# Out-projection operands built inside the last attention turn, and two output tiles started on their attention half, in a hybrid attention and state-space decoder step

## The reference, cut to what matters

```
att = att_fn(q, k, v, qi, wi, ki)
...
y = rmsnorm(y.reshape(B, T, SSM_WIDTH) * jax.nn.silu(z), ssm_norm)
h = x + jnp.concatenate([att, y], axis=-1) @ w_out
f = rmsnorm(h, norm_ffn)
h = h + (jax.nn.silu(f @ w_gate) * (f @ w_up)) @ w_down
```

## Time and profile before

| | |
|---|---|
| median of 3 runs | 3020.83 us (3015.36 to 3022.0) |
| the profiled execution | 3024.53 us, span 3022.4 us |
| PE busy | 2830.1 us (94%) |
| DVE, ACT, POOL busy | 1508.8, 949.1, 548.8 us |
| turn 8 and start of the out-projection | about 1120 to 1223 us of the span |
| DMA | 354.00 MB, mean 117 GB/s |

### The profile page before, as it was taken

The page is one execution under the profiler, slowest core; times in us unless marked ns, Lnnn a source line. Parts: engine busy times, 40 slices in busy tenths (PEclk is TensorE's granted clock), DMA queues, the critical chain, the costliest instruction groups (busy, mean ns, idle before and its releaser), DMA issues.

```text
span 3022.4 us, 49649 instructions
## 1 busy us (share of the span) xinstructions
PE 2830.1 (94%) x20713; PEld 2694.1 (89%) x20713; DVE 1508.8 (50%) x2311; ACT 949.1 (31%) x1440; POOL 548.8 (18%) x230
## 2 busy tenths in 40 slices
PE   6999999999999986997899999999999999999997
PEld 5887898877777764996899999999999999999997
DVE  3312399544444445015766776766766633232223
ACT  4222221232333323223334344343333422222222
POOL 2222232211111100431000000000000033333331
PEclk9999999999999987998899999999999999999999
DMA  6422222555555545442232333333333352323221
GB/s 203 115 72 73 72 77 78 147 150 159 158 148 150 152 119 189 131 131 80 78 110 96 128 100 98 121 100 115 105 100 119 116 200 100 115 100 116 100 100 63
DMA packets 367372, 354.00 MB, mean 117 GB/s; under 512 B 40957, under 2 KB 321125, under 8 KB 365880
## 3 DMA queue, kind: packets, MB, share of 16 engines
q1 hardware_dynamic: 334136, 325.20, 34.0%
q10 hardware_dynamic: 33024, 25.77, 2.6%
HBM read 303.18 MB, written 49.13 MB: 117 GB/s over the span
## 4 chain that ended last, share of the span: by engine, by line
PE 57%; issue 31%; POOL 7%; DVE 2%; ACTq 1%; ACT 1%; POOLq 0%; DVEq 0%
PE PS L1230 32%; PE PS L1212 19%; PE PS L789 6%; POOL WL L692 4%; POOL WL L721 3%; ACTq L1274 0%; DVE XR L2264 0%; ACTq L1275 0%; DVE xo_t L2269 0%; DVE xo_x L2269 0%; DVE y_out L2339 0%; POOL WL L713 0%; ACT WRAW L1283 0%; DVE rstd L2257 0%; PE PS L804 0%
## 5 line engine op out<-in xcount | busy, mean ns | idle before, releaser
L789 PE MATMUL PS<-AH,WH 128*128 128x288 f32 (+1 forms) x2208 | 497.6, 308 | 30.1 <-DVE AL L2164 11.0
L1212 PE MATMUL PS<-H,WH 128*128 128x288 f32 x2816 | 489.5, 296 | 0.7 <-DVE us L2231 0.7
L789 PE MATMUL PS<-AL,WH 128*128 128x288 f32 (+1 forms) x2208 | 483.8, 302 | 0.0
L789 PE MATMUL PS<-AH,WL 128*128 128x288 f32 (+1 forms) x2208 | 482.3, 301 | 0.0
L711 POOL TENSOR_TENSOR WL<-WRAW,WH 128x1024 fp32r<-128x1024 f32 x88 | 213.9, 2431 | 1379.6 <-ACT WH L704 1379.6
L789 PEld LDWEIGHTS PS<-AH,WH 128*128 128x128 f32 (+1 forms) x2208 | 366.8, 195 | 56.4 <-issue 35.1
L1212 PEld LDWEIGHTS PS<-H,WH 128*128 128x128 f32 x2816 | 414.6, 189 | 0.9 <-issue 0.9
L1230 PE MATMUL PS<-xo_t,WH 128*128 128x288 f32 x1888 | 380.9, 296 | 7.8 <-ACT kept L1627 7.6
L789 PEld LDWEIGHTS PS<-AL,WH 128*128 128x128 f32 (+1 forms) x2208 | 367.0, 194 | 0.0
L789 PEld LDWEIGHTS PS<-AH,WL 128*128 128x128 f32 (+1 forms) x2208 | 365.5, 194 | 0.0
L2325 DVE TENSOR_TENSOR XD<-PS,XD 128x576 f32<-128x576 f32 x176 | 133.4, 758 | 398.8 <-PE PS L1212 398.8
(11 more groups left out here) (351 smaller groups left out, 3786.2 us busy)
## 6 DMA issues: line engine op xcount, KB each, us to landing
WRAW<-in_w_gate SPq DMA_DIRECT2D x22, 2048.0 KB
WRAW<-in_w_up SPq DMA_DIRECT2D x22, 2048.0 KB
WRAW<-in_w_down SPq DMA_DIRECT2D x22, 2048.0 KB
WRAW<-in_w_in SPq DMA_DIRECT2D x14, 2048.0 KB, 8.4
raw<-in_w_in SPq DMA_DIRECT2D x48, 512.0 KB, 4.1
kca<-in_cache_k SPq DMA_DIRECT2D x256, 64.0 KB, 2.8
vca<-in_cache_v SPq DMA_DIRECT2D x256, 64.0 KB, 2.0
WRAW<-in_w_out SPq DMA_DIRECT2D x16, 1024.0 KB
```

The source lines that it names most:

```text
L789: last = nc.tensor.matmul(G[gslot][0:width, h, 0:HALF], wt[:, half, k % 8, 0:width], act[:, (k + shift) % KT, h * HALF:(h + 1) * HALF], st ...
L1212: last = mm(G[(slot + t) % 2][:, h, 0:HALF], wt[:, half, 2 * k + t, :], hid[:, m, k, h * HALF:(h + 1) * HALF], start=(k == 0 and wt is WH ...
```

## The change

`mx` gets 16 places and lies where `AL` lies, so each low part is written over its own input. That memory is free once the last q, k, v product has been read (`w_used` at C3). In turn 8, SP issues two loads of seven rows each, attention rows 0 to 6 and SSM rows 8 to 14, between values 3 and keys 2. Rows 15 and 7 are loaded singly after the turn. ACT (`mix_high`) and DVE (`mix_low`) build the parts of rows 0 to 6 inside turn 8. After the turn ACT makes the first two weight halves, then row 7's high part, then the root, then rows 8 to 15. PE computes the attention halves of tiles 0 and 1 first, and then their SSM halves, as `ATT_FIRST` says.

```
-        mx = sb("mx", [P, 6, NT], at=spot["bf"][0])
+        mx = sb("mx", [P, KT, NT], at=spot["AL"][0])
...
+        ATT_FIRST = (0, 2, 1, 3)
...
+            def load_mix(n, lo, hi):
+                sp.dma_start(mx[:, lo:hi, :], mixS[lo:hi].rearrange("k p n -> p k n")).then_inc(mx_in[n], 16)
...
             def turn_sp(i, att=True, units=True, mamba=True, more=True):
                 a = i - 1
                 for n in range(6):
+                    if n == 2 and not units:
+                        sp.wait_ge(s["w_used"], C3)
+                        sp.wait_ge(s["mixa"], 16 * 7)
+                        load_mix(0, 0, 7)
+                        sp.wait_ge(s["ymix"], 16 * 7)
+                        load_mix(1, 8, 15)
...
             sp.wait_ge(s["hout"], 16 * 8)
             load_w(0, out_cols(0), 0)
             sp.wait_ge(s["ymix"], 16 * 8)
+            load_mix(3, 15, 16)
+            twait(sp, "pvs", 8)
+            load_w(1, out_cols(1), 1)
+            sp.wait_ge(s["mixa"], 16 * NH)
+            load_mix(2, 7, 8)
...
-            sp.wait_ge(s["mixa"], 16 * 7)
-            for j in range(6):
-                load_mix(j)
-            twait(sp, "pvs", 8)
-            load_w(1, out_cols(1), 1)
...
-            for j in range(6, KT):
-                load_mix(j)
...
-            for n in range(KT):
+            for d, (n, h) in enumerate(((0, 0), (1, 0), (0, 1), (1, 1))):
+                if d < 2:
+                    pe.wait_ge(s["tile_taken"], T3 + n - 1)
+                ready = (lambda k: pe.wait_ge(s["mix_lo"], k + 1)) if n == 0 else None
+                half_unit(pe, C3 + d, h, (T3 + n) % 2, ready=ready, slot=d % 2)
+            for n in range(2, KT):
...
+            def mix_high(j):
+                act.wait_ge(mx_in[{7: 2, 15: 3}.get(j, j // 8)], 16)
+                if j >= 8:
+                    act.wait_ge(s["y_norm"], j - 7)
+                copy(AH[:, j, :], mx[:, j, :]).then_inc(s["m_hi"], 1)
...
-            hi_p(C3, 0, 0)
-            hi_p(C3 + 1, 1, 0)
...
+            hi_p(C3, 0, 0, 0)
+            hi_p(C3 + 1, 2, 0, 1)
+            mix_high(7)
+            for h in range(2):
+                wait(act, f"ssy{h}")
+                taken(actv(rstd[:, h, :], bank(f"ssy{h}")[:, 0:HALF], ACT.Sqrt, bias=eps[:, :], scale=1.0 / (NM * DS)), f"ssy{h}")
+            for j in range(8, KT):
+                mix_high(j)
...
             for c in range(2, 32):
-                hi_p(C3 + c, c % 4, c // 4)
+                if c < 4:
+                    hi_p(C3 + c, ATT_FIRST[c], 0, c % 2)
+                else:
+                    hi_p(C3 + c, c % 4, c // 4)
...
+            def mix_low(j):
+                dve.wait_ge(s["m_hi"], j + 1)
+                tt(AL[:, j, :], mx[:, j, :], AH[:, j, :].bitcast(F32), ALU.subtract).then_inc(s["mix_lo"], 1)
...
+            mix_low(7)
+            for h in range(2):
+                given(dve, f"ssy{h}")
+            dve.wait_ge(s["tile_taken"], T3)
+            nc.vector.reciprocal(rstd[:, :, :], rstd[:, :, :]).then_inc(s["ry_done"], 1)
+            dve.wait_ge(s["ry_done"], 1)
+            for j in range(8, KT):
+                y_norm(j)
+                if j > 8:
+                    mix_low(j - 1)
+            mix_low(KT - 1)
```

More of the change, by code:

```diff
@@ L242, in build @@
         w_ld = [sem(f"w_ld{t}") for t in range(2)]
-        mx_in = [sem(f"mx_in{t}") for t in range(6)]
+        mx_in = [sem(f"mx_in{t}") for t in range(4)]
         xt_in = [sem(f"xt_in{t}") for t in range(2)]
@@ L586, in out_cols @@
                 return src
[L588 to L594, removed]
             def load_x(n):
@@ L699, in as_down, with upper_p @@
             return w[:, half, :, :].rearrange("p (k t) c -> p k (t c)", t=2)
-        def upper_p(act, c, h, f, down):
+        def upper_p(act, c, h, f, down, slot=None):
             act.wait_ge(s["w_used"], c - 1)
-            if down:
+            if slot is not None:
+                nc.scalar.copy(WH[:, slot, :, :], raw_pair((1, 0)[f % 2], h // 2)[:, 8 * (h % 2):8 * (h % 2) + 8, :]).then_inc(s["w_hi"], 1)
+            elif down:
                 nc.scalar.copy(as_down(WH, h % 2), w_down_half((1, 0)[f % 2], h)).then_inc(s["w_hi"], 1)
@@ L770, in _ @@
                     lower8(pool, 6 * i + 58 + n, raw3[:, n % 3, :, :], n % 2)
-            with pool.Fori(0, 4) as i:
+            for h in range(4):
+                lower_p(pool, C3 + h, ATT_FIRST[h], 0, False, h % 2)
+            for h in range(4):
+                lower_p(pool, C3 + 4 + h, h, 1, False)
+            with pool.Fori(1, 4) as i:
                 for f in range(2):
@@ L779, in _, with half_unit @@
                         lower_p(pool, 8 * g + (CD + 4 * f + h), h, f, True)
-        def half_unit(pe, c, half, gslot, width=P, shift=0, ready=None):
+        def half_unit(pe, c, half, gslot, width=P, ready=None, slot=None):
             pe.wait_ge(s["w_lo"], c + 1)
@@ L788, in half_unit @@
                     for h in range(2):
-                        last = nc.tensor.matmul(G[gslot][0:width, h, 0:HALF], wt[:, half, k % 8, 0:width], act[:, (k + shift) % KT, h * HALF:(h + 1) * HALF],
+                        last = nc.tensor.matmul(G[gslot][0:width, h, 0:HALF], wt[:, half if slot is None else slot, k % 8, 0:width], act[:, k, h * HALF:(h + 1) * HALF],
                                                 start=(k == 0 and wt is WH and act is AH), stop=(k == KT - 1 and wt is WL))
@@ L1501, in turn_act @@
                     hi3(i, 4)
+                else:
+                    mix_high(0)
                 if att:
@@ L1512, in turn_act @@
                     hi3(i, 5)
+                else:
+                    mix_high(1)
+                    mix_high(2)
                 if att:
@@ L1531, in turn_act @@
                     hi3(i + 1, 0)
+                if not units:
+                    mix_high(3)
+                    mix_high(4)
                 if att:
@@ L1551, in turn_act @@
                     exp_logits(i, 4)
+                if not units:
+                    mix_high(5)
+                    mix_high(6)
                 if mamba:
@@ L1568, in _, with hi_p @@
             turn_act(8, units=False)
[L1569 to L1574, removed]
+            def hi_p(c, h, f, slot=None):
                 if h == 0:
                     act.wait_ge(w_ld[f % 2], 4 * (c - C3 - 4 * (f % 2)) + 32)
-                upper_p(act, c, h, f, down)
+                upper_p(act, c, h, f, False, slot)
             def token_sums(m):
@@ L2107, in turn_dve @@
                         take(i, 1, kT)
+                    if c == 2 and not units:
+                        mix_low(0)
+                        mix_low(1)
+                        mix_low(2)
                 if mamba:
@@ L2138, in turn_dve @@
                     take(i, 2, vT)
+                else:
+                    for j in range(3, 7):
+                        mix_low(j)
                 if att:
@@ L2153, in y_norm @@
             def y_norm(j):
-                v = mx[:, j % 6, :]
-                dve.wait_ge(mx_in[j % 6], 16 * (j // 6 + 1))
+                v = mx[:, j, :]
+                dve.wait_ge(mx_in[3 if j == 15 else 1], 16)
                 stt(v, v, gains[:, 24 + j:25 + j], rstd[:, :, :].rearrange("p a b -> p (a b)"), ALU.mult, ALU.mult).then_inc(s["y_norm"], 1)
[L2157 to L2168, removed]
+            mix_low(7)
[9 more added lines that the diff above has]
+            mix_low(KT - 1)
             two = lambda v: v.rearrange("p (a b) -> p a b", a=2)
```

14 lines of the change are left out of this document (8 added, 6 removed).

## The result

| | before | after |
|---|---|---|
| median, same chip, 5 runs each | 3018.83 us (3015.36 to 3022.0) | 3032.9 us (3025.15 to 3035.02) |
| ratio, 95% interval | | 1.0043 [1.0031, 1.0055] |
| the profiled execution, its span | 3024.53 us, 3022.4 us | 3035.02 us, 3033.0 us |
| PE busy | 2830.1 us (94%) | 2821.7 us (93%) |

The change made the kernel slower by 0.43% (0.31 to 0.55%), which is 13.0 us of 3018.8. The forecast was +13.7 us and 3034.5 us; it started from the 3020.8 us that three runs of before had given.

The account below looks back on a forecast made before the run. PE, busy 94% of the span, was taken to bound the kernel. 10.9 + 0.2 + 0.3 + 2.3 = +13.7 us raised the profiled 3024.53 us to 3038.2, median 3034.5 us; range 3021.5 to 3041.

Parts of the forecast that it names:

- Step 1: Turn 8: the two large loads on SP's queue delay keys 2 by 12.3 us; cost +10.9 us to the turn's end.
- the 1.4 us to be made up: SP's queue in turn 8: keys 3 are transposed while keys 4 are issued, so a wait goes, recovering 1.4 us.
- rival (a): Turn 8: the keys aren't held by the large loads; +2.8 us remain, 3023.6 us; chance 0.14.
- Step 2: Casts on ACT and subtractions on DVE within turn 8: mostly covered by waits, +0.2 us; weight load 1.4 us later.
- Step 3: After turn 8: row 7 lands late with the root behind it; net +0.3 us at weight half 2.
- One sign: First matmul of the out-projection: comes about 8 us after the `attT` store is issued, on a wait for `WL`.
- Step 4: Out-projection: PE idles after the two attention halves, then runs 4.7 us at 1.2 GHz instead of 2.4; +2.3 us.
- (b): After turn 8: faster, row 7 lands before 1188 us and weight half 2 comes 5.5 us sooner; 3015.3 us; chance 0.06.
- (c): Worse: at 307 GB/s keys and row 7 come later, PE's small matmuls run at 0.50 longer; 3042 us; chance 0.16.

Follow-up runs that it names:

- Half the bytes: Changed kernel with only rows 0 to 6 loaded in turn 8 and rows 8 to 14 loaded behind row 7 after the turn; ratio 1.0020 [1.0008, 1.0032].
- late loads: Changed kernel with both large loads after values 7, casts of rows 0 to 6 after the last `pt` copy, row 7 before the second weight pair; ratio 0.9991.
- row 7 first: Changed kernel with row 7 of `mixS` loaded ahead of the second weight pair; ratio 1.0026 [1.0013, 1.0040], or 1.0003 [0.9992, 1.0014] with the root first too.
- the third: Changed kernel with large loads after values 7, row 7 and root early, weight half 2's high part made behind row 12's; median 3007.86 us, 0.36% below before.
- the second and fourth: Changed kernel with large loads after values 7, row 7 and root early; the fourth also has the old order of halves; 0.26% and 0.30% below before.

## Why the prediction was right

The sign, the place and nearly the size held: +13.7 us foreseen, +13.0 [9.4, 16.6] measured, and the median 1.6 us under the forecast. Part of that closeness is luck. The profiled pair, on which the steps can be checked, gives +11.7 us in the three pieces and +10.6 us of span.

**Step 1** foresaw a wait of about 13 us and +10.9 us to the end of the turn. The wait was 12.04, and A grew by 10.5. Half the bytes halved the loss, and late loads removed it. But two misses cancel in the 10.9. Counted from the start of A, keys 2 were transposed 10.7 us later than before, not 12.3: SP reached the large loads 0.7 us sooner, and keys 2 came 14.85 us after their issue instead of the 15.8 that 376 GB/s gives. The measured 417 GB/s gives 14.6. And the 1.4 us to be made up because SP's wait for a free `kca` buffer goes were not made up that way. That wait grew, before and then with the change (total us, times, longest):

```profile
SPq L516 <- PE PS L974: 1.6, 2, 1.3
SPq L517 <- PE PS L983: 5.8, 1, 5.8
```

SP had issued keys 2 and 3 by 1144.01 us and could go on only at 1149.97, once keys 2 were transposed. Up to keys 4 PE made up 1.2 us, as a wait of 1.40 us for DVE's `els` went, and it lost 1.0 us again to the later keys 4 to 7.

The figure of the Trainium skill (DMA: Bandwidth & Descriptors, section Bandwidth), 425 GB/s for a 16 MB load, was nearer to the 417 GB/s here than my row. Its forecast of 3033.1 us lies 0.2 us from the median, but against the measured change of +13.0 us both (+12.3 and +13.7) are 0.7 us off, so the time doesn't decide between them.

**The reason given for step 1 was too narrow.** I wrote that "what SP issues late lands after everything it issued before", and held against rival (a) that row 6 fits a strict order. That speaks of one queue. The load on ACT's queue showed that keys on the other queue wait nearly as long. What fits these runs is the bytes already outstanding while the DMA engines are full (share 1.03 to 1.07), not the queue that they came by. Rival (a) failed, but the order in SP's ring isn't shown to be the cause. The prediction would have been as good for a change that used ACT's queue, for a reason that it didn't give.

**Step 2** was +0.2 us, and B is 0.2 us longer, but not where the step put it, so the match is luck. The three subtractions before `take_y(i, 3)` ended 0.15 us before PE's result came. PE's wait for `lgs` is what grew, from 2.76 to 2.96 us; why isn't shown. That `hout` would come 1.4 us later was wrong: the `ssm_sample` store went out at 1176.25 us, 10.6 us before the `attT` store, against 10.46 before. The two casts stand ahead of it in the program, but their row is at 1176.92 us: ACT's queue issued the DMA while the casts, behind the exponential of 1176.15 us, had yet to run. The weight loads, which wait for this store, went out 6.6 us before the `attT` store (before: 6.45).

**Step 3** expected the third half 33.4 us after the `attT` store (before 33.1). It came after 32.27, so the term of +0.3 us was really -0.8. What was mis-sized is the time of the weight issue, which step 2 had made 1.4 us late: it was put 5.1 us before the store and came 6.6 before. From the weight issue on the terms fit. Row 7 was cast 17.9 us after it (17.6 foreseen, with 376 GB/s for the 5.09 MB), and the weights were usable after 9.74 us, as before. So row 7 was cast 11.25 us after the store instead of 12.5, and the first half began 6.7 us after it instead of 8.1. The chain itself (row 7, table load, root, reciprocal, norms, weight half, POOL) stands row by row as foreseen. One sign can't be read as written: the profile puts the wait before the first half to "issue" and not to `WL`, though POOL had made that half's low part just before (from 1191.11 us, two in 4.67 us).

**Step 4** was +2.3 us. PE idled 10.01 us, started at clock 0.50, and began a pair of matmuls every 0.48 us instead of every 0.27 from 1219.14 to about 1223.1 us: eight pairs in 4.0 us where 2.1 would do, 1.9 us lost. The stretch to the taking of tile 2 shows the same, 27.74 and 27.48 us with the new order against 25.92 with the old. "The reordering of halves brings nothing" was thus still kind to it. Steps 3 and 4 together foresaw +2.6 us, and C grew by 1.0: -0.8 to the third half, +1.8 behind it.

**Rivals (b) and (c).** For (b) row 7 would have had to land before 1188 us in the old clock. It was cast at 1188.0 in that clock (11.25 us after a store at 1176.77), at the very edge of its condition, and still nothing was gained, because keys 2 had cost 10.5 us first. Of (c), the 307 GB/s didn't occur in the burst of turn 8, whose windows shown here have 369 and 400. The small matmuls after the gap did run at the low clock (1.09 us for four transposes instead of 0.63), within A.

## What to carry to other kernels

A prefetch isn't free because the DMA engines look half idle. If small loads that PE needs at once come behind it, they can wait for nearly all of its bytes, and another queue need not help (here 4.13 MB cost 7 to 11 us, whichever queue had them). Place it where nothing urgent follows. And once operands come early, ask what then sets the start: here it was the last row to arrive, in front of a root that didn't need it. Moving the root ahead again took 5.5 us off C in the changed kernel and 6.4 with the late loads, while the new order of the halves brought nothing in any of them.

## What the runs showed of the hardware that was not expected

**B, the end of turn 8, varies between traces.** It was 22.5 to 22.9 us in six of them (before, after, before with the new order, row 7 first with and without the root first, eight DMAs on ACT's queue), 23.8 to 24.0 in three, and 27.6 to 31.3 in the other five. The four kernels with late loads have other code in B than after, but the same among themselves; yet the third has 23.80 us where the second and fourth have 29.39 and 29.55. The changed kernel with the old order has the code of after in B, and 31.29 us. The sixteen small matmuls of L1021, and all of B as a stretch, with the old order in the changed kernel; then B in after:

```profile
1158.69 3.42 PE L1021 MATMUL PS<-cf,hTb 128*128 128x8 f32 x16
```

```profile
1157.59:1188.88 31.29, 25.37 (x138) 17.43 (x139) 12.89 (x30) 6.28 (x17) 0.00 (x0) 0.50 0.38 116
```

```profile
1164.12:1186.87 22.75, 16.54 (x138) 11.59 (x139) 12.72 (x30) 6.18 (x17) 0.00 (x0) 0.82 0.49 151
```

In after the sixteen took 1.85 us. The same 138 matmuls ran at a granted clock of 0.50 throughout in one trace and of 0.82 on average in the other. The five long traces are 5 to 9 us above the short ones, more than most of the effects studied here. It is why the table leaves B out, and why single traces can't be compared by their span. What decides which execution falls into it stays open.

**A DMA can be issued ahead of work that is written before it.** This is the `ssm_sample` store of step 2: issued at 1176.25 us, with two casts of its own engine, written ahead of it, running from 1176.92.

**SP issues small loads more slowly behind a burst.** The eight loads of keys 2 and 3 took SP 9.05 us to issue behind fourteen rows, and 4.28 behind seven; eight key loads took 3.95 before. The rest of the 19.32 us for sixteen is mostly the wait of 5.8 us for a free `kca` buffer (6.2 with seven rows, of 14.99 in all). Why the issuing slows isn't shown.
